# Turning the feed-forward activations by in-quadrant transposes and an exchange of quadrants over DMA

## The reference, cut to what matters

```
h2 = rms_norm(x, norm_ffn_g)
u = square(relu(h2 @ w_up))      # 2048 x 8192
x = x + u @ w_down               # 8192 x 2048
return rms_norm(x, norm_final_g)
```

## Time and profile before

| | |
|---|---|
| median of 3 runs | 1476.74 us (1476.65 to 1477.01) |
| profiled execution | 1476.18 us, span 1474.4 us |
| PE busy in the span | 99% |
| DVE, ACT busy in the span | 81%, 52% |
| mean granted TensorE clock | 0.999 |
| DMA | 299.33 MB, 203 GB/s |

### The profile page before, as it was taken

One profiled execution on the slowest core, in us unless ns is written; L12 is line 12 of the kernel. 1 busy time (PEld: TensorE's weight loads), 2 busy tenths in 40 slices (PEclk: granted clock), 3 DMA queues, 4 the chain that ended last, 5 costly groups with the idle time before them and its releaser, 6 DMA issues.

```text
span 1474.4 us, 18772 instructions
## 1 busy us (share of the span) xinstructions
PE 1465.7 (99%) x6968; PEld 1279.8 (87%) x6968; DVE 1190.9 (81%) x1558; ACT 766.8 (52%) x986; POOL 15.0 (1%) x21
## 2 busy tenths in 40 slices
PE   9999999999999999999999999999999999999997
PEld 8888888888888888888888888888888888888886
DVE  7977887776577788777799988888897888889877
ACT  7656565444455555444445555555554555555553
POOL 0000000000000000000000000000000000000000
PEclk9999999999999999999999999999999999999999
DMA  9556544667655566556765665656666656655563
GB/s 333 191 169 211 184 154 164 229 203 241 213 180 184 186 199 206 194 200 200 248 233 181 202 219 201 218 185 207 217 204 202 208 199 226 214 199 193 198 209 114
DMA packets 149801, 299.33 MB, mean 203 GB/s; under 512 B 5232, under 2 KB 5360, under 8 KB 149488
## 3 DMA queue, kind: packets, MB, share of 16 engines
q1 hardware_dynamic: 149168, 297.51, 59.9%
q10 hardware_dynamic: 576, 1.06, 0.2%
HBM read 296.45 MB, written 2.10 MB: 202 GB/s over the span
## 4 chain that ended last, share of the span: by engine, by line
PE 98%; issue 1%; DVE 1%; POOLq 0%; POOL 0%; DVEq 0%; ACT 0%
PE acc L545 88%; PE acc L827 3%; PE banks L776 3%; PE acc L776 1%; PE banks L564 1%; PE banks L583 1%; PE banks L573 0%; PE banks L591 0%; DVE ta_lo L1775 0%; PE banks L680 0%; PE banks L696 0%; PE banks L695 0%; PE banks L693 0%; PE acc L603 0%; DVE final L1787 0%
## 5 line engine op out<-in xcount | busy, mean ns | idle before, releaser
L865 ACT ACTIVATE whi<-raw 128x1024 fp32r<-128x1024 f32 x542 | 569.2, 1056 | 577.3 <-PE acc L545 517.9
L1222 DVE TENSOR_TENSOR wlo<-raw,whi 128x1024 fp32r<-128x1024 f32 x542 | 655.1, 1223 | 213.1 <-ACT whi L865 208.5
L545 PE MATMUL acc<-whi,ta_hi 128*128 128x512 f32 x1308 | 497.4, 380 | 0.0
L545 PE MATMUL acc<-wlo,ta_hi 128*128 128x512 f32 x1308 | 495.7, 379 | 0.0
L545 PE MATMUL acc<-whi,ta_lo 128*128 128x512 f32 x1308 | 495.7, 379 | 0.0
L545 PEld LDWEIGHTS acc<-whi,ta_hi 128*128 128x128 f32 x1308 | 247.2, 189 | 36.7 <-issue 1.2
L545 PEld LDWEIGHTS acc<-whi,ta_lo 128*128 128x128 f32 x1308 | 247.2, 189 | 35.1
L545 PEld LDWEIGHTS acc<-wlo,ta_hi 128*128 128x128 f32 x1308 | 247.3, 189 | 34.5
L545 PE MATMUL acc<-whi,tb_hi 128*128 128x512 f32 x560 | 212.3, 379 | 0.0
L545 PE MATMUL acc<-wlo,tb_hi 128*128 128x512 f32 x560 | 212.2, 379 | 0.0
L545 PE MATMUL acc<-whi,tb_lo 128*128 128x512 f32 x560 | 212.2, 379 | 0.0
(11 more groups left out here) (208 smaller groups left out, 1049.2 us busy)
## 6 DMA issues: line engine op xcount, KB each, us to landing
raw<-in_w_in SPq DMA_DIRECT2D x64, 1024.0 KB, 5.2
raw<-in_w_up SPq DMA_DIRECT2D x64, 1024.0 KB, 5.3
raw<-in_w_down SPq DMA_DIRECT2D x57, 1024.0 KB, 5.0
raw<-in_w_gate SPq DMA_DIRECT2D x32, 1024.0 KB, 5.3
raw<-in_w_att SPq DMA_DIRECT2D x16, 1024.0 KB, 5.0
raw<-in_w_ret SPq DMA_DIRECT2D x16, 1024.0 KB, 5.0
raw<-in_w_out SPq DMA_DIRECT2D x16, 1024.0 KB, 5.0
raw<-in_w_down SPq DMA_DIRECT2D x14, 512.0 KB, 4.3
```

The source lines that it names most:

```text
L545: last = nc.tensor.matmul(paired(acc[B.parity][:, t, :]), a[:, k, tok], halves_in_turn(b), start=(k == 0 and n == 0), stop=(k == (B.ends + ...
L865: nc.scalar.activation(whi[:, B.ring_at(u), :], raw[:, B.raw_at(u), :], ACT.Copy).then_inc(hi_ready, 1)
L1222: V_.tensor_tensor(wlo[:, at, :], raw[:, B.raw_at(u), :], whi[:, at, :].bitcast(f32), ALU.subtract).then_inc(lo_ready, 1)
```

## The change

`buf[0]` is turned by four transposes over all 128 partitions, for o = 0 to 3: the squares of 32 x 32 in columns o*32 to o*32+31 of each chunk are transposed, each within its own 32 partitions (a quadrant), into `buf[3]`. When the four are done (`quads_turned`), SP issues 16 transfers from `buf[3]` to `buf[1]`, one for each pair of quadrants: 32 rows of 1 KB from quadrant i to quadrant o. Each counts 16 on `exchanged`. ACT and DVE read the result through views with runs of 32 elements and wait for 256 on `exchanged` per turn. The order on DVE becomes: splits 0 to 3, four transposes, splits 4 to 7 (or 4 and 5 and two of `B[5]`), lo in two halves. On SP the exchange stands between the second and the third load of the block behind `B[i]`. ACT's `squared_relu` waits for `quads_turned` in place of `t_full`; `mixed_tokens` waits for `exchanged` and reads the new views.

```diff
+        in_quads = buf[3][:].rearrange("p t (o n) -> p (t o) n", n=S)
+        exchanged_at = buf[1][:].rearrange("p t (i n) -> p (t i) n", n=S).rearrange("p i (a n) -> p i a n", n=SQ)
+        by_block = exchanged_at.rearrange("p i a n -> p a i n")
+        by_tile = exchanged_at.rearrange("p i (m t) n -> p m t i n", t=TILES)
...
+            def exchange(n):
+                sp.wait_ge(quads_turned, n)
+                for i in range(QUADS):
+                    for o in range(QUADS):
+                        sp.dma_start(exchanged_at[o * SQ:(o + 1) * SQ, i].rearrange("f a n -> f (a n)"),
+                                     in_quads[i * SQ:(i + 1) * SQ, o, :]).then_inc(exchanged, 16)
...
-                for i in range(1, 4):
-                    load_block(B[i], w_up, q * D + i * COLS)
-                for i in range(2):
-                    load_rows(B[4 + i], w_down, i * COLS, q * D, range(4 if last else 3))
+                load_block(B[1], w_up, q * D + COLS)
+                for i in range(2, 4):
+                    load_rows(B[i], w_up, q * D + i * COLS, 0, range(2))
+                    exchange(q * 4 + (i - 1))
+                    load_rows(B[i], w_up, q * D + i * COLS, 0, range(2, 4))
+                load_rows(B[4], w_down, 0, q * D, range(2))
+                exchange(q * 4 + 3)
+                load_rows(B[4], w_down, 0, q * D, range(2, 4 if last else 3))
+                load_rows(B[5], w_down, COLS, q * D, range(2 if last else 3))
+                exchange(q * 4 + 4)
+                if last:
+                    load_rows(B[5], w_down, COLS, q * D, range(2, 4))
...
-                        act.wait_ge(t_full, q * 4 + (T_STAGE6 + i - 1))
+                        act.wait_ge(quads_turned, q * 4 + (i - 1))
...
-                    hi_from_turned(q * 4 + (T_STAGE6 + i - 1), tb_hi, i - 1)
+                    hi_from_exchanged(q * 4 + i, i - 1)
...
+            def hi_from_exchanged(n, g):
+                act.wait_ge(exchanged, n * TURNED)
+                for h in range(2):
+                    to = tb_hi[:, g * GCH + h * UCH:g * GCH + (h + 1) * UCH, :].rearrange("p m (t i n) -> p (m t) i n", t=TILES, n=SQ)
+                    nc.scalar.activation(to, by_block[:, h * GCH:(h + 1) * GCH], ACT.Copy).then_inc(t_hi, 1)
...
-                    turn_among(B[i], q * 4 + (T_STAGE6 + i - 1), buf[0][:], u_ready, q * 4 + i, ((4, 0, 10), (5, 10, 14)))
-                    short = i == 4 and not last
-                    rest = (lambda n: split(B[5], n, n + 1)) if short else (lambda n: split(B[i], 6 + n, 7 + n))
-                    rest(0)
-                    lo_from_turned(q * 4 + (12 + i), tb_hi, tb_lo, i - 1)
-                    rest(1)
+                    dve.wait_ge(u_ready, q * 4 + i)
+                    for o in range(QUADS):
+                        last_piece = V_.transpose(in_quads[:, o, :].rearrange("p (m t n) -> p m t n", t=TILES, n=SQ),
+                                                  by_chunk(buf[0][:])[:, :, :, o * SQ:(o + 1) * SQ])
+                    last_piece.then_inc(quads_turned, 1)
+                    split(B[i], 4, B[i].ends + 1)
+                    if i == 4 and not last:
+                        split(B[5], 0, 2)
+                    lo_from_exchanged(q * 4 + (12 + i), i - 1)
...
+            def lo_from_exchanged(n, g):
+                for h in range(2):
+                    dve.wait_ge(t_hi, n * 2 + (h - 1))
+                    hi, lo = [a[:, g * GCH + h * UCH:g * GCH + (h + 1) * UCH, :].rearrange("p m (t i n) -> p (m t) i n", t=TILES, n=SQ)
+                              for a in (tb_hi, tb_lo)]
+                    V_.tensor_tensor(lo, by_block[:, h * GCH:(h + 1) * GCH], hi.bitcast(f32),
+                                     ALU.subtract).then_inc((first_half, t_free)[h], 1)
...
-                dve.wait_ge(t_full, q * 4 + (T_STAGE6 + 4))
+                dve.wait_ge(exchanged, q * (4 * TURNED) + 4 * TURNED)
```

More of the change, by code:

```diff
@@ L335, in build @@
         product_done, folded = sem("product_done"), sem("folded")
+        quads_turned, exchanged = sem("quads_turned"), sem("exchanged")
         final_g, final_act, final_dve, stored = sem("final_g"), sem("final_act"), sem("final_dve"), sem("stored")
@@ L355, in build @@
         turned = buf[1][:].rearrange("p t (m n) -> p (t m) n", n=S)
+        QUADS = P // SQ
+        TURNED = QUADS * QUADS * 16
+        in_quads = buf[3][:].rearrange("p t (o n) -> p (t o) n", n=S)
+        exchanged_at = buf[1][:].rearrange("p t (i n) -> p (t i) n", n=S).rearrange("p i (a n) -> p i a n", n=SQ)
+        by_block = exchanged_at.rearrange("p i a n -> p a i n")
+        by_tile = exchanged_at.rearrange("p i (m t) n -> p m t i n", t=TILES)
         tokens = [slice(t * P, (t + 1) * P) for t in range(TILES)]
@@ L1730, in mixed_tokens @@
             def mixed_tokens(q):
-                dve.wait_ge(t_full, q * 4 + (T_STAGE6 + 4))
-                (a11, a21), (a12, a22) = [[turned[:, half, tokens[t]] for t in range(TILES)] for half in (slice(0, UCH), slice(UCH, GCH))]
-                V_.tensor_tensor(mixed[:, 0], a21, a22, ALU.subtract).then_inc(mixed_set, 1)
-                V_.tensor_tensor(mixed[:, 1], a11, a21, ALU.subtract).then_inc(mixed_set, 1)
+                dve.wait_ge(exchanged, q * (4 * TURNED) + 4 * TURNED)
+                (a11, a21), (a12, a22) = [[by_tile[:, half, t] for t in range(TILES)] for half in (slice(0, UCH), slice(UCH, GCH))]
+                m = [mixed[:, c].rearrange("p k (i n) -> p k i n", n=SQ) for c in range(MIXED)]
+                V_.tensor_tensor(m[0], a21, a22, ALU.subtract).then_inc(mixed_set, 1)
+                V_.tensor_tensor(m[1], a11, a21, ALU.subtract).then_inc(mixed_set, 1)
                 dve.wait_ge(mixed_set, q * MIXED + 1)
-                V_.tensor_tensor(mixed[:, 2], mixed[:, 0], a11, ALU.subtract).then_inc(mixed_set, 1)
+                V_.tensor_tensor(m[2], m[0], a11, ALU.subtract).then_inc(mixed_set, 1)
                 dve.wait_ge(mixed_set, q * MIXED + 3)
-                V_.tensor_tensor(mixed[:, 3], mixed[:, 2], a12, ALU.add).then_inc(mixed_set, 1)
+                V_.tensor_tensor(m[3], m[2], a12, ALU.add).then_inc(mixed_set, 1)
             def first_two_sums(G):
```

## The result

The kernel after takes 1481.74 us (median of 8 runs, 1480.40 to 1483.51) against 1476.68 of the kernel before in the same runs: ratio 1.0035, 95% interval 1.0024 to 1.0046. It is 5.1 us slower, which is more than the 0.2% that such a measurement tells from no change. The profiled execution took 1483.37, its span is 1481.6, 7.2 more than before's.

The account below looks back on a forecast made before the run. PE was taken to bound the kernel, with unbroken matmuls in the feed-forward stage: 0 for the freed DVE time plus a 0.4 us stall gave 1476.6, or 1477.1 as median; own range 1476.2 to 1478.6, extended up to 1483.

Parts of the forecast that it names:

- the first rival: SyncE's issues too slow in the exchange: from a 0.65 us pitch every turn stalls PE; 1517 at 0.8; chance 0.08.
- The likeliest case: Whole kernel: time within 0.2% (3.0 us) of the kernel before, chance 0.80.
- What is removed: DVE's transposes in the feed-forward stage: 5.2 us freed a turn, 84 us in all, worth 0 for the end.
- The pitch of the issues: SyncE's 16 issues in the exchange: 0.46 us apart, bounds 0.42 and 0.50, far end 1.23; 6.9 us for 15 pitches.
- Issue to landing: A 32 KB transfer of the exchange: 2.0 us, taken between 1.6 and 2.6; all sixteen landed at 1399.1.
- The DMA engines' room: DMA engines in the last turn's block: idle from about 1392.0 to 1397.7, enough for 512 packets, 3.0 us at most.
- SyncE's loads: Third load of the next block, behind the 16 issues on SyncE's queue: issued at 1397.6, hidden by 5.2 us.
- the strided views: Copies and subtractions for hi and lo on strided views: change 0, at most 0.05 us a piece.
- The last turn: PE at unit 6 of the last turn's block: first half of lo at 1400.5, needed at 1400.12, one 0.4 us stall.
- An ordinary turn: 15 of 16 turns: no PE stall, 2.8 us of room; landing may come as late as 17.3 us into the block.
- The signs: Right: ACT waiting 2.7 us a turn, break under 2 us near 1400; wrong: sixteenth landing over 11.7 us after the last transpose.
- Two or three units later ACT waits for PE again: ACT in the block behind an ordinary turn: its lateness from the exchange is gone within two or three units.

Follow-up runs that it names:

- e_first_three: Kernel after, but with the new path in quarters 0 to 2 only, the last quarter turning as the kernel before does: 1479.29 us, ratio 1.0019.
- e_late_fourth: Kernel after, with hi and lo of the fourth turn made later by ACT and DVE in quarters 0 to 2: 1480.79 us, ratio 1.0025.
- e_last_only: Kernel after, but with the new path in the last quarter only, the others turning as the kernel before does: 1479.31 us, ratio 1.0022.
- p_issues: Kernel after plus seven groups of transfers on SyncE's queue behind the last store, to read issue length and landing; its time says nothing.
- e_pool: Kernel after, with eight of the sixteen transfers issued by GpSimd on its own queue and semaphore: 1482.54 us, ratio 1.0040.
- e_twenty: Kernel after, with the four transfers from quadrant 0 cut in two halves, twenty transfers of the same bytes: 1520.98 us, ratio 1.030.

## Why the prediction came out as it did

The time was inside the range, but not for the forecast's reason. The forecast's own range, 1476.2 to 1478.6, and its stall of 0 to 1.6 us were missed: 1481.74, and 2.3 at the last turn. The range went up to 1483 only to take in the edge of the first rival, issues too slow, and half of the loss came from a place that the prediction did not look at. The likeliest case, no measurable change, was not what came: it was 5.1 us, and slower had a chance of 0.18. That the number lies inside is in part luck.

- What is removed: right. 64 transposes of 0.413 (bounds 0.436 and 1.74), DVE 89 us less busy, worth nothing for the end. So the four quadrants together take no longer than one; that fits the independent blocks of the Trainium skill ("VectorE: DVE Perf Modes", "The three transpose paths").
- The pitch of the issues: the term that was mis-sized. 0.46 was taken, with 0.50 as the near bound; 0.63 was measured in the last turn, up to 0.69 in others. Every row of issues that the prediction drew on was of transfers from HBM. The nearest row was near in place and in order, and far in the one thing in which the long issues differ: both ends in SBUF. That is 15 x 0.17 = 2.6 us on the landing. Of that 0.3 came back ahead of the first issue and 0.2 from the time to land, and the stall grew from 0.4 to 2.3.
- Issue to landing: 2.0 taken, 1.9 measured. The estimate from rows was near, and so is the fixed 2.0 us of the Trainium skill ("DMA: Bandwidth & Descriptors", "Anatomy of one DMA"), which it has for another queue than SyncE's.
- The DMA engines' room, SyncE's loads, the strided views: right, all nothing (1476.50 with everything but the wait).
- The last turn: the working holds, with the true landing. 1404.27 + 0.03 + 0.62 + 0.03 + 0.70 is 1405.65, and PE goes on at 1405.70; it was due at 1403.5.
- An ordinary turn: right, and narrowly. In the kernel after the landings came 16.2 to 17.3 us behind the first matmul of the block; the prediction's point, 17.3 behind its first weight load, is 17.1 so counted. PE lost 0.1 us once, behind the landing at 17.3 (the third turn of quarter 0), and 0.3 in e_first_three and in e_late_fourth behind landings at 17.5; at 17.2 it lost nothing. Twenty transfers went beyond the point in every turn, and PE waited 25.3 us there against 24 worked out.
- The signs: ACT stood 5.0 us a turn and not 2.7 (79.6 in all and not 43), the break near 1400 was over 2 us, and in five of the sixteen turns the last landing came 11.75 to 12.2 us behind the last transpose, past the 11.7 that was to count as wrong.
- "Two or three units later ACT waits for PE again": true of ACT and of the turns that a block of plain splits follows, false of the fourth. I followed the queue behind the wait for one block only, and took the fourth turn of a quarter for one of "15 of 16". Behind it DVE has 30 us with hardly an idle time, and a load on SyncE's queue waits for it. That is 2.6 us, half of the loss.
- The clock: not in the prediction. The stall of the last turn was followed by 3.4 us at half clock, 1.7 us more, in the profiled executions of the kernel after and of e_late_fourth and not in that of e_last_only. By the mean clocks it is in two of the eight runs of the kernel after, so it is no part of the 5.1 us.
- Of the rivals, the slow issues were the nearest: 0.63 lies just below the 0.65 from which the prediction had every turn stall, and just below it the prediction had 3.2 us, at the last turn alone. The last turn's 2.3 fit that; the 2.6 in quarters 0 to 2 don't, and no rival had them.

No version here beats the kernel before. Its matmuls run without a break until 1447; a path that is never late, like twelve transfers, ends at the same 1476.70.

## What to carry to other kernels

When work is moved from a busy engine to a chain of small DMAs and the busy engine isn't what sets the end, the best that can come is nothing, and the risk is latency: count the issues, take their pitch from transfers with the same two ends, and add it up. Where an engine waits in its queue, follow what stands behind the wait up to the next place where it is idle, over loads that depend on it too; slack that one block has may be missing in the next. Here, leaving out the transfers that don't cross anything gave back all of the 5.1 us, and issuing the first before the last input is ready 3.7.

## What the runs showed of the hardware

- SyncE needed 0.59 to 0.60 us for an issue from SBUF to SBUF in a row of them (0.625 with 8 rows of 4 KB), 0.42 to 0.43 from HBM to SBUF (p_issues). In three of the sixteen turns of the kernel after one issue took 1.5. GpSimd needed 0.498 for the same 32 KB from SBUF to SBUF, beside SyncE's (e_pool).
- A transfer of 32 KB from SBUF to SBUF on SyncE's queue landed 1.9 us behind its issue (median of 256, 1.7 at least).
- In e_pool, the one kernel in which GpSimd issued transfers, GpSimd reached the closing barrier 5.6 us behind SyncE's last DRAIN; in the kernels before and after it was under 0.05.
- A transpose of 128x256 took 0.413 us (kernel after), one of 32x256 took 0.436 (kernel before).
- PE's clock fell to 1.2 GHz behind some stalls: behind idle times of 2.1 us in the kernel after and in e_late_fourth and of 2.3, 2.6 and 4.8 in e_twenty (0.50 to 0.57 granted, for 3.4 us, for 6.8 behind the last), and not behind the one of 2.1 in e_last_only nor behind shorter ones.
